# Square and column scaling of the gated SSD rows moved from GpSimd to ScalarE in a hybrid decoder step

## The chip, the cores and the metric

One Trainium2 chip, one core of it. The metric is the device time of one execution in microseconds (us), lower is better. The engines are TensorE (PE in the rows), VectorE (DVE), ScalarE (ACT), GpSimd (POOL) and SyncE (SP), each with its own instruction queue; they meet at semaphores.

## What is computed

One inference step of a one-layer decoder, for a prompt of 256 tokens and 8 samples of 8 new tokens each, so 320 columns in all: a Mamba-2 branch beside a chunked MLP branch, a gated merge, and a mixture of 32 experts (top 4). The change touches the gated norm between the Mamba-2 branch and its output weights:

```python
def rmsnorm(x, w):
    xf = x.astype(jnp.float32)
    y = xf * lax.rsqrt(jnp.mean(xf * xf, axis=-1, keepdims=True) + EPS)
    return (y * w.astype(jnp.float32)).astype(x.dtype)

y_ssd, new_ssm = ssd_chunked(xs, dt, a_log, b_ssm, c_ssm, ssm_init)   # 32 heads of 64 channels
y_ssd = y_ssd + d_skip[:, None] * xs
y_ssd = rmsnorm(y_ssd.reshape(bsz, l, D_INNER) * jax.nn.silu(z), gnorm_w)
merged = g_ssd * (y_ssd @ w_branch_ssd) + g_mlp * (y_mlp @ w_branch_mlp)
h = x + merged @ w_out
```

Everything is float32. Weights and activations of the mixer are split into a rounded high part (fp32r) and the rest, and multiplied as three products.

## The kernel before

**Stages.** The kernel runs on one core in one program. From 0 to about 118 us it norms and turns the input and projects the first column tiles. The pair stage (about 118 to 369 us) handles the 32 heads as 16 pairs of 128 channels, j = 0 to 15, in four groups g of four; jj = j % 4. The branch stage follows (L1189 on), in which the MLP and SSD branches meet their weights, then the output projection, the router, and from about 600 us the experts, whose weights stream in on SyncE's queue. SyncE issues the first expert loads when all eight merged tiles are there (L597).

**Layout.** Channels lie on the 128 partitions and the 320 tokens along the row. yT holds 16 tiles of 128x320: first silu(z), then, multiplied in place, the gated y of pair j. The norm over channels needs the sum of the squares of all 16 tiles, kept in sqacc (128x320), which one matmul with ones adds up over the partitions after the last pair (L1211). The norm's weight is a column per tile, gn_col[:, j].

**One pair.** The order of every engine's queue is written out by hand. TensorE (L1159 to L1187) makes the heads' cumulated decays (heads, L1083), turns the input states (turn_state, in two halves), multiplies the diagonal block of the pair before, makes chunk states, new states (L1136) and the off-diagonal part (offT), and between these the halves of two or three projection tiles that the table beside(j) names (half_tile: L900 to L909): convolution tiles, z tiles, in the last group u tiles and a gate. The heads of pair j wait for the head decays of pair j-1 (e_ready) and its sample states (sn_ready). ScalarE (L1839 to L1870) reads the last tile of the pair before (late), then copies states (L1769), takes the exponentials (read_heads, exponent), copies chunk states (L1778, L1781), makes the high part of the late tile's weights (L1628), issues the stores of the states and the load of the input states for pair j+1 (store_states, on ScalarE's own DMA queue), copies offT (L1861) and reads the next tiles: for a convolution tile raw (L1688, L1689) and a scaled copy (L1691). VectorE (L2364 to L2385) makes the segments of pair j (L2307), the gated y of pair j-1 (gated, L2338 to L2342), the convolution of the late tile (three taps, a 128x256 and a 128x64 step each, L2222 and L2224), the weighted x (L2276), the low part of the late weights (L2086), the sample states (L2319), and further convolutions. The low part of a weight tile is made four tiles ahead of its use by TensorE (split_lo).

**GpSimd** (L785 to L800) masks the decays of pair j (decay, L756, 128x640), then handles pair j-1's y in squares (L759): square (L763 or L765), sum into sqacc (L766), and y times the norm's column in place (L767), chained by semaphores. Then it packs the convolution rows (L734, L735), copies prefixes (L723) and in each group stores rows by its own DMA queue. After the last pair it waits for the partition sum and issues the router's and biases' loads.

**After the pairs** ScalarE makes the high parts of the operands in the order of BRANCH (L522): the MLP rows, weight 2, four quarters of y, the other weights (split_high, L1818, copies at L1836). Quarter i of y waits for sq_ready at 4i+4, since its rows must be scaled before they are split. VectorE makes the low parts in the same order (split_low, L2362).

Of the kernel before, what the change touches and what calls it, by code (L numbers as in the profile page):

```python
# [12 lines left out]
ALU = mybir.AluOpType  # L13
# [16 lines left out]
PAIRS = DI // P  # L30
# [90 lines left out]
def build(nc, x_prompt, x_sample, state_conv, state_ssm, norm_mix, w_in, conv_w, conv_b, dt_bias, a_log,  # L121
# [4 lines left out]
    with ctx:  # L126
# [160 lines left out]
        def part(*shape):  # L287

            n = 1
            for d in shape:  # L290
# [76 lines left out]
                 "sT_psum", "sT_ready", "s0_ready", "sf_psum", "sf_ready", "sn_psum", "sn_ready",  # L367
                 "off_psum", "off_read", "yd_psum", "y_ready", "sq_ready", "sq_psum", "rs_var", "rs_std",
                 "rs_ready", "gates_ready", "merged", "out_psum", "h_ready", 
# [285 lines left out]
        def _(pool):  # L655
# [102 lines left out]

            def squares(j):  # L759

                pool.wait_ge(S["y_ready"], j + 1)
                if j == 0:
                    link(pool.tensor_tensor(sqacc, yT[:, j, :], yT[:, j, :], ALU.mult))  # L763
                else:
                    link(pool.tensor_tensor(sq, yT[:, j, :], yT[:, j, :], ALU.mult))  # L765
                    link(pool.tensor_tensor(sqacc, sqacc, sq, ALU.add))  # L766
                pool.tensor_scalar(yT[:, j, :], yT[:, j, :], gn_col[:, j:j + 1], None, ALU.mult  # L767
                                   ).then_inc(S["sq_ready"], 1)

# [15 lines left out]
            for j in range(PAIRS):  # L785
                convs = [n for kind, n in beside(j) if kind == "conv"]
                if convs:
                    prefix_of(convs[0])
                if j % 4 == 0:
                    mask_b(j // 4)  # L790
                decay(j)
                if j:
                    squares(j - 1)
                for i, n in enumerate(convs):
                    if i:
                        prefix_of(n)
                    pack_of(n)
                if j % 4 == 0:
                    store_rows(j // 4)
            squares(PAIRS - 1)  # L800
            pool.wait_ge(s_new_out[0], 16 * PAIRS // 2)
# [802 lines left out]
        def _(act):  # L1604
# [178 lines left out]
            def exponent(j):  # L1783
# [4 lines left out]
                fn(dec, seg, ACT.Exp).then_inc(S["exp_ready"], 1)  # L1788

            def store_states(j):  # L1790

# [26 lines left out]
            def split_high(item):  # L1818
# [8 lines left out]
                if kind == "y":  # L1827
                    act.wait_ge(s_new_out[0], 16 * PAIRS // 2)
                    act.wait_ge(s_new_out[1], 16 * PAIRS // 2)
                    act.wait_ge(s_fin_out[0], 16 * PAIRS // 2)  # L1830
                    act.wait_ge(s_fin_out[1], 16 * PAIRS // 2)
                    act.wait_ge(S["yd_psum"], PAIRS)
                    act.wait_ge(S["sq_ready"], 4 * i + 4)
                if kind == "mlp":
# [4 lines left out]
            for j in range(PAIRS):  # L1839
# [10 lines left out]
                read_state(j, 1)  # L1850
                read_chunk_states(j)
                if jj >= 2 and after_g < G:
                    read_rows(after_g, jj - 2)
# [33 lines left out]
            for item in BRANCH:  # L1887
                kind, i = item
                split_high(item)
                if item == ("w", 4):  # L1890
                    act.wait_ge(S["rs_var"], 1)
                    act.sqrt(rstd_row, rstd_row).then_inc(S["rs_std"], 1)
                if kind == "w" and i % 5 == 2:
# [170 lines left out]
        def _(dve):  # L2064
# [336 lines left out]
            for item in BRANCH:  # L2401
# [4 lines left out]
                if item == ("w", 4):  # L2406
                    dve.wait_ge(S["sq_psum"], 1)
                    dve.tensor_scalar(rstd_row, bank[0][:, 0:T], 1.0 / DI, EPS, ALU.mult, ALU.add
                                      ).then_inc(S["rs_var"], 1)
                    dve.wait_ge(S["rs_std"], 1)  # L2410
                    dve.reciprocal(rstd_row, rstd_row).then_inc(S["rs_ready"], 1)
                    dve.wait_ge(S["rs_ready"], 1)
# [345 lines left out]
```

## Time and profile before

| | |
|---|---|
| median of 3 runs | 1535.34 us (1534.7 to 1537.41) |
| the profiled execution | 1537.08 us |
| its span in the trace | 1535.2 us |
| TensorE busy | 1424.8 us (93%) |
| VectorE busy | 602.3 us (39%) |
| ScalarE busy | 381.1 us (25%) |
| GpSimd busy | 202.4 us (13%), 303 instructions |
| mean granted TensorE clock | 0.981 of full speed |
| chain that ended last | PE 60%, DMA 25%, DVE 8%, ACT 1%, POOL 1% |

The span runs from the first to the last instruction; 1.9 us lie around it. The profiled execution is 1.7 us above the median of the runs. In the rows, idle time before an instruction is that of its own engine, and the releaser is the instruction whose semaphore came last. Start times are us from the span's start. In merged rows (xN) the length is that of the N instructions together.

### The profile page before, as it was taken

What the parts mean: (1) busy time and instruction counts of PE and PEld (TensorE: products, weight loads), DVE (VectorE), ACT (ScalarE), POOL (GpSimd) and SP (SyncE); (2) the same over time, 40 slices, a digit from 0 to 9 for tenths busy, and PEclk for the clock granted to TensorE, in tenths of its full rate; (3) what the DMA queues carried; (4) which work ended last, traced back from release to release, by engine and by line L of the source; (5) the groups of instructions that cost most, each with busy time, mean ns of one, the idle gap of its engine ahead of it and who ended that gap; (6) DMA issues with size and microseconds to landing.
All of it is one profiled execution on the core that took longest, in us unless ns stands there. A gap on an engine that the chain in (4) does not pass through costs nothing.

```text
span 1535.2 us, 22060 instructions
## 1 busy us (share of the span) xinstructions
PE 1424.8 (93%) x8519; PEld 830.7 (54%) x8520; DVE 602.3 (39%) x1348; ACT 381.1 (25%) x642; POOL 202.4 (13%) x303
## 2 busy tenths in 40 slices
PE   5999999999999999989999899987999989999996
PEld 4988788788999544434434434432434434434432
DVE  4796888967544152312212212202212113112213
ACT  4556676756332141001001001000000001001002
POOL 4023444335930000000000000000000000000000
PEclk9999999999999999999999999998999999999999
DMA  7443554555444879999999999997999999999996
GB/s 225 147 136 112 145 166 124 170 154 158 148 155 151 328 290 387 427 428 429 427 429 428 429 428 429 428 427 290 406 429 428 429 428 429 428 429 429 429 422 238
DMA packets 127406, 495.85 MB, mean 323 GB/s; under 512 B 7300, under 2 KB 95420, under 8 KB 102200
## 3 DMA queue, kind: packets, MB, share of 16 engines
q1 hardware_dynamic: 89152, 471.75, 76.0%
q10 hardware_dynamic: 35888, 18.88, 4.2%
q0 software_dynamic: 2304, 4.40, 1.0%
q8 instruction: 40, 0.66, 0.2%
q14 instruction: 22, 0.18, 0.0%
HBM read 483.65 MB, written 11.34 MB: 322 GB/s over the span
## 4 chain that ended last, share of the span: by engine, by line
PE 60%; DMA 25%; DVE 8%; issue 3%; SPq 2%; ACT 1%; POOL 1%; DVEq 0%; ACTq 0%; POOLq 0%
DMA ring_b<-in_w_gu 23%; PE bank L1405 18%; PE bank L1488 9%; PE bank L1227 7%; PE bank L1342 3%; PE bank L900 3%; PE bank L909 3%; PE bank L881 3%; PE bank L1243 2%; PE bank L905 2%; PE bank L902 1%; DVE ring_r L2086 1%; SPq L583 1%; DVE arena L2222 1%; DVE arena L2224 1%
## 5 line engine op out<-in xcount | busy, mean ns | idle before, releaser
L1405 PE MATMUL bank<-ring_b,xe 128*64 128x512 f32 x1248 | 346.2, 618 | 36.6 <-DMA ring_b<-in_w_gu 36.5
L1405 PEld LDWEIGHTS bank<-ring_b,xe 128*64 128x64 f32 x1248 | 113.9, 142 | 253.3 <-issue 252.6
L1405 PE MATMUL bank<-ring,xe 128*64 128x512 f32 x768 | 226.0, 594 | 5.0 <-DMA ring<-in_w_gu 4.7
L1488 PE MATMUL bank<-ring,actT 128*64 128x512 f32 x720 | 213.0, 596 | 0.0
L1608 ACT ACTIVATE swi<-swi 128x256 f32<-128x256 f32 x66 | 27.3, 416 | 560.5 <-DVE swi L2535 528.1
L2535 DVE TENSOR_SCALAR swi<-bank 128x256 f32<-128x256 f32 x60 | 25.5, 425 | 314.5 <-PE bank L1405 309.7
L1227 PE MATMUL bank<-rounded,ring_r 128*128 128x320 f32 x912 | 133.7, 308 | 1.7 <-DVE ring_r L2362 1.7
L1227 PEld LDWEIGHTS bank<-rounded,ring_r 128*128 128x128 f32 x912 | 132.8, 188 | 2.6 <-DVE ring_r L2362 2.4
L853 POOL TENSOR_TENSOR kept<-take 128x256 bf16<-128x256 bf16 x15 | 9.2, 612 | 855.2 <-PE bank L1470 855.2
L1405 PEld LDWEIGHTS bank<-ring,xe 128*64 128x64 f32 x768 | 74.6, 137 | 76.4 <-issue 76.4
L1488 PE MATMUL bank<-ring_b,actT 128*64 128x512 f32 x240 | 105.8, 593 | 4.3 <-ACT actT L1970 4.3
L2576 DVE TENSOR_TENSOR hid<-hid,bank 128x512 f32<-128x512 f32 (+1 forms) x90 | 57.8, 682 | 115.0 <-PE bank L1366 115.0
L1488 PEld LDWEIGHTS bank<-ring,actT 128*64 128x64 f32 x720 | 64.6, 137 | 59.1 <-issue 58.8
L900 PE MATMUL bank<-rounded,ring_r 128*128 128x320 f32 x456 | 84.1, 328 | 0.6 <-ACT rounded L1634 0.6
L909 PE MATMUL bank<-rounded,ring_r 128*128 128x320 f32 x456 | 76.6, 310 | 0.0
L2086 DVE TENSOR_TENSOR ring_r<-ring,ring_r 128x1024 fp32r<-128x1024 f32 (+1 forms) x61 | 73.7, 1222 | 3.5 <-ACT ring_r L1628 3.3
L881 PE MATMUL bank<-ident,arena 128*128 128x128 f32 (+5 forms) x337 | 55.8, 285 | 19.0 <-DVE arena L2079 17.8
L900 PEld LDWEIGHTS bank<-rounded,ring_r 128*128 128x128 f32 x456 | 70.5, 196 | 3.6 <-issue 2.3
L909 PEld LDWEIGHTS bank<-rounded,ring_r 128*128 128x128 f32 x456 | 69.8, 189 | 0.0
L2669 DVE SCALAR_TENSOR_TENSOR ye_lo<-bank,routing,ye_hi 128x512 fp32r<-128x512 f32 x32 | 22.6, 747 | 115.4 <-ACT ye_hi L1981 105.7
L1488 PEld LDWEIGHTS bank<-ring_b,actT 128*64 128x64 f32 x240 | 31.6, 137 | 60.6 <-issue 60.6
L1628 ACT CAST ring_r<-ring 128x1024 fp32r<-128x1024 f32 (+1 forms) x61 | 63.4, 1041 | 1.6 <-ACT arena L1608 1.0
(371 smaller groups left out, 2016.4 us busy)
## 6 DMA issues: line engine op xcount, KB each, us to landing
ring_b<-in_w_gu SPq DMA_DIRECT2D x79, 2048.0 KB, 16.5
ring<-in_w_gu SPq DMA_DIRECT2D x49, 2048.0 KB, 16.7
ring<-in_w_down SPq DMA_DIRECT2D x47, 2048.0 KB, 18.7
ring<-in_w_in SPq DMA_DIRECT2D x32, 1024.0 KB, 5.4
ring_b<-in_w_down SPq DMA_DIRECT2D x15, 2048.0 KB, 14.4
arena<-in_state_ssm ACTq DMA_DIRECT2D x16, 512.0 KB, 4.7
out<-arena ACTq DMA_DIRECT2D x16, 512.0 KB, 3.6
ring<-in_w_branch_ssd SPq DMA_DIRECT2D x8, 1024.0 KB, 5.2
```

Of the source, the lines that this page charges most:

```text
L881: return pe.transpose(out, in_, ident[0:in_.shape[0], 0:in_.shape[0]])
L900: pe.matmul(o, w_h[k], hn_hi[:, k, :], start=(k == 0), stop=False)
L905: pe.matmul(o, w_l[k], hn_hi[:, k, :], start=False, stop=False)
L909: mm = pe.matmul(o, w_h[k], hn_lo[:, k, :], start=False, stop=(k == KD - 1))
L1227: mm = pe.matmul(bank[4 * m + b][:, 0:T], w[:, k, m * P:m * P + P], v[:, k0 + k, :], start=(k == 0 and which != 4 and v is x_h and w is w_ ...
L1243: mm = pe.matmul(bank[2 * half + c][:, :], mergedT[:, 2 * m + k, tok(c)], w[:, k, hb(c, half)], start=(m == 0 and k == 0), stop=(m == 3 an ...
L1342: mm = pe.matmul(bank[6 + k // 4][:, (k % 4) * P:(k % 4) * P + P], part[0:rows(c), c, k * P:k * P + P], chosen_rows[0:rows(c), c, :], star ...
L1405: mm = pe.matmul(bank[q][side(h), :], xe[:, j, side(h)], moe_slot(2 * i + h, first)[:, 2 * FF * k + 512 * q:2 * FF * k + 512 * q + 512], s ...
L1488: mm = pe.matmul(bank[4 + half][side(h), :], actT[:, f, side(h)], w[:, D * k + 512 * half:D * k + 512 * half + 512], start=False, stop=(f ...
L1628: act.copy(hi, w).then_inc(S["split_hi"], 1)
L2086: dve.tensor_tensor(lo, w, hi.bitcast(F32), ALU.subtract).then_inc(S["split_lo"], 1)
L2576: dve.tensor_tensor(hid[0:rows(c), c, hb(c, half)], hid[0:rows(c), c, hb(c, half)], bank[6 + i % 2][0:rows(c), :], ALU.add).then_inc(S["cm ...
```

## The change

ScalarE makes the square of pair j's gated y and its scaling by the norm's column (square_y). GpSimd keeps the decay mask and the sum (add_squares). The square of pair 0 is written straight to sqacc. ScalarE's instruction for pair j-1 stands in pair j behind its chunk states; that of pair 15 stands ahead of the high part of the last quarter of y. ScalarE waits for GpSimd's sum of the pair before, since sq has one buffer, and for its own square before it scales in place. GpSimd waits for both. The square root of the norm uses the count of another semaphore pair (ln_var, ln_std) in place of its own.

```diff
--- before.py
+++ after.py
@@ -365,7 +365,7 @@
                  "cb_psum", "cb_ready", "bt_psum", "bt_ready", "bm_ready", "xt_psum", "xw_ready",
                  "head_psum", "seg_ready", "exp_ready", "decay_ready", "e_ready", "ident_ready", "mlp_ready",
                  "sT_psum", "sT_ready", "s0_ready", "sf_psum", "sf_ready", "sn_psum", "sn_ready",
-                 "off_psum", "off_read", "yd_psum", "y_ready", "sq_ready", "sq_psum", "rs_var", "rs_std",
+                 "off_psum", "off_read", "yd_psum", "y_ready", "sq_ready", "sq_psum", "y_squared",
                  "rs_ready", "gates_ready", "merged", "out_psum", "h_ready", 
                  "lg_psum", "lg_ready", "ge_ready", 
                  "split_hi", "split_lo", "cnt_psum", "rank_psum", "work_ready", 
@@ -756,16 +756,14 @@
                 pool.tensor_tensor(dec, dec, cbm.unsqueeze(1).to_broadcast([P, 2, T]), ALU.mult
                                    ).then_inc(S["decay_ready"], 1)
 
-            def squares(j):
-
-                pool.wait_ge(S["y_ready"], j + 1)
-                if j == 0:
-                    link(pool.tensor_tensor(sqacc, yT[:, j, :], yT[:, j, :], ALU.mult))
+            def add_squares(j):
+
+                pool.wait_ge(S["y_squared"], 2 * j + 2)
+                if j:
+                    pool.wait_ge(S["sq_ready"], j)
+                    pool.tensor_tensor(sqacc, sqacc, sq, ALU.add).then_inc(S["sq_ready"], 1)
                 else:
-                    link(pool.tensor_tensor(sq, yT[:, j, :], yT[:, j, :], ALU.mult))
-                    link(pool.tensor_tensor(sqacc, sqacc, sq, ALU.add))
-                pool.tensor_scalar(yT[:, j, :], yT[:, j, :], gn_col[:, j:j + 1], None, ALU.mult
-                                   ).then_inc(S["sq_ready"], 1)
+                    pool.sem_inc(S["sq_ready"], 1)
 
             def store_rows(g):
 
@@ -790,14 +788,14 @@
                     mask_b(j // 4)
                 decay(j)
                 if j:
-                    squares(j - 1)
+                    add_squares(j - 1)
                 for i, n in enumerate(convs):
                     if i:
                         prefix_of(n)
                     pack_of(n)
                 if j % 4 == 0:
                     store_rows(j // 4)
-            squares(PAIRS - 1)
+            add_squares(PAIRS - 1)
             pool.wait_ge(s_new_out[0], 16 * PAIRS // 2)
             pool.wait_ge(s_new_out[1], 16 * PAIRS // 2)
             pool.wait_ge(s_fin_out[0], 16 * PAIRS // 2)
@@ -1787,6 +1785,15 @@
                     act.wait_ge(S["yd_psum"], j)
                 fn(dec, seg, ACT.Exp).then_inc(S["exp_ready"], 1)
 
+            def square_y(j):
+
+                act.wait_ge(S["y_ready"], j + 1)
+                if j:
+                    act.wait_ge(S["sq_ready"], j)
+                fn(sq if j else sqacc, yT[:, j, :], ACT.Square).then_inc(S["y_squared"], 1)
+                act.wait_ge(S["y_squared"], 2 * j + 1)
+                act.mul(yT[:, j, :], yT[:, j, :], gn_col[:, j:j + 1]).then_inc(S["y_squared"], 1)
+
             def store_states(j):
 
                 p = j % 2
@@ -1830,6 +1837,8 @@
                     act.wait_ge(s_fin_out[0], 16 * PAIRS // 2)
                     act.wait_ge(s_fin_out[1], 16 * PAIRS // 2)
                     act.wait_ge(S["yd_psum"], PAIRS)
+                    if i == 3:
+                        square_y(PAIRS - 1)
                     act.wait_ge(S["sq_ready"], 4 * i + 4)
                 if kind == "mlp":
                     act.wait_ge(S["mlp_ready"], KD)
@@ -1849,6 +1858,8 @@
                     read_b(j // 4)
                 read_state(j, 1)
                 read_chunk_states(j)
+                if j:
+                    square_y(j - 1)
                 if jj >= 2 and after_g < G:
                     read_rows(after_g, jj - 2)
                 if j:
@@ -1888,8 +1899,8 @@
                 kind, i = item
                 split_high(item)
                 if item == ("w", 4):
-                    act.wait_ge(S["rs_var"], 1)
-                    act.sqrt(rstd_row, rstd_row).then_inc(S["rs_std"], 1)
+                    act.wait_ge(S["ln_var"], 4)
+                    act.sqrt(rstd_row, rstd_row).then_inc(S["ln_std"], 1)
                 if kind == "w" and i % 5 == 2:
                     gates_of("gs", i // 5)
                 if kind == "w" and i % 5 == 3:
@@ -2406,8 +2417,8 @@
                 if item == ("w", 4):
                     dve.wait_ge(S["sq_psum"], 1)
                     dve.tensor_scalar(rstd_row, bank[0][:, 0:T], 1.0 / DI, EPS, ALU.mult, ALU.add
-                                      ).then_inc(S["rs_var"], 1)
-                    dve.wait_ge(S["rs_std"], 1)
+                                      ).then_inc(S["ln_var"], 1)
+                    dve.wait_ge(S["ln_std"], 4)
                     dve.reciprocal(rstd_row, rstd_row).then_inc(S["rs_ready"], 1)
                     dve.wait_ge(S["rs_ready"], 1)
             merge(3)
```

## Rows read from the trace of the kernel before

**Rows 1.** Busy us by stage (PE, PEld, DVE, ACT, POOL); clock, DMA share, GB/s.

```profile
300.00:350.00 50.00, 48.38 (x366) 42.00 (x366) 36.55 (x98) 30.17 (x51) 17.48 (x19) 0.97 0.52 154
...
600.00:1535.00 935.00, 855.45 (x4602) 353.88 (x4598) 215.69 (x489) 76.26 (x159) 14.43 (x30) 0.98 0.98 414
```

**Rows 2.** Timeline, TensorE: start, us, engine, line, operation [idle before, releaser].

```profile
178.39 0.52 PE L1083 MATMUL bank<-rounded,rounded 64*128 64x320 f32 x2 [1.64 <-issue]
...
291.40 0.53 PE L1083 MATMUL bank<-rounded,rounded 64*128 64x320 f32 x2 [0.27 <-issue]
...
296.96 0.40 PE L881 MATMUL bank<-ident,arena 128*27 128x128 f32 x2 [0.20 <-ACT arena L1608]
...
306.73 0.53 PE L1083 MATMUL bank<-rounded,rounded 64*128 64x320 f32 x2 [1.62 <-issue]
```

**Rows 3.** Timeline, VectorE, pairs 8 (alone) and 10.

```profile
257.25 0.48 DVE L2222 SCALAR_TENSOR_TENSOR arena<-arena 128x256 f32<-128x256 f32 x1
257.65 0.28 DVE L2224 SCALAR_TENSOR_TENSOR arena<-arena 128x64 f32<-128x64 f32 x1
...
282.58 1.58 DVE L2224 SCALAR_TENSOR_TENSOR arena<-arena 128x64 f32<-128x64 f32 x1
284.19 0.84 DVE L2222 SCALAR_TENSOR_TENSOR arena<-arena 128x256 f32<-128x256 f32 x1
...
285.88 0.78 DVE L2222 SCALAR_TENSOR_TENSOR arena<-arena 128x256 f32<-128x256 f32 x1
...
291.23 0.47 DVE L2222 SCALAR_TENSOR_TENSOR arena<-arena 128x256 f32<-128x256 f32 x1
```

**Rows 4.** Timeline, all engines, end of the pairs.

```profile
373.36 2.81 DVE L2362 TENSOR_TENSOR ring_r<-ring,ring_r 128x2048 fp32r<-128x2048 f32 x1
...
377.00 3.53 POOL L767 TENSOR_SCALAR arena<-arena 128x320 f32<-128x320 f32 x1
380.64 1.26 ACT L1836 CAST rounded<-arena 128x1280 fp32r<-128x1280 f32 x1 [3.35 <-POOL arena L767]
...
381.93 1.49 DVE L2362 TENSOR_TENSOR rounded<-arena,rounded 128x1280 fp32r<-128x1280 f32 x1 [0.62 <-ACT rounded L1836]
...
383.74 2.29 DVE L2362 TENSOR_TENSOR ring_r<-ring,ring_r 128x2048 fp32r<-128x2048 f32 x1 [0.32 <-ACT ring_r L1836]
...
386.09 21.25 PE L1227 MATMUL bank<-rounded,ring_r 128*128 128x320 f32 x144 [0.80 <-DVE ring_r L2362]
```

**Rows 5.** GpSimd by line, 118 to 382 us: busy, mean ns, idle.

```profile
L767 POOL TENSOR_SCALAR arena<-arena 128x320 f32<-128x320 f32 x16 | 24.4, 1523 | 1.6
...
L765 POOL TENSOR_TENSOR arena<-arena 128x320 f32<-128x320 f32 x15 | 13.3, 887 | 5.4 <-DVE arena L2342 5.4
```

**Rows 6.** Timeline, ScalarE, pairs 9 and 10.

```profile
272.02 0.37 ACT L1861 COPY arena<-bank 128x256 f32<-128x256 f32 x1 [1.02 <-PE bank L1148]
...
273.95 0.37 ACT L1688 COPY arena<-bank 128x256 f32<-128x256 f32 x1 [0.24 <-PE bank L909]
...
290.03 0.63 ACT L1608 ACTIVATE arena<-bank,arena 128x320 f32<-128x320 f32 x1
```

**Rows 7.** Busy time behind the gaps, pairs 4 and 12, as rows 1.

```profile
178.39:183.48 5.09, 5.09 (x41) 4.31 (x42) 4.53 (x14) 3.26 (x5) 0.00 (x0) 1.00 0.72 194
...
306.73:313.32 6.59, 6.59 (x41) 5.42 (x42) 4.62 (x14) 3.26 (x5) 0.00 (x0) 0.74 0.46 156
```

**Rows 8.** ScalarE by line, 118 to 370 us; line 1981: minimum, median, maximum.

```profile
L1608 ACT ACT_TABLE_LOAD x30 | 38.5, 1283 | 0.5
L1769 ACT COPY arena<-bank 128x512 f32<-128x512 f32 x31 | 18.2, 586 | 23.3 <-PE bank L881 22.8
...
L1608 ACT ACTIVATE arena<-arena 128x320 f32<-128x320 f32 x18 | 7.8, 467 | 0.1
...
L1981 ACT ACTIVATE ye_hi<-bank,routing x30: 680/684/687, 605.5 to 1466.5; 128x512 fp32r<-128x512 f32 x30
```

**Rows 9.** DMA issues of the page: KB each, us from issue to landing.

```profile
arena<-in_state_ssm ACTq DMA_DIRECT2D x16, 512.0 KB, 4.7
```

## The prediction, made before the changed kernel ran

> **What bounds the kernel now.** I read the busy times by stage first. From 600 us on the DMA engines are busy 0.98 of the time at 414 GB/s, so that stage is as long as its bytes and only its start can move. In the pair stage (about 118 to 369 us) no DMA bound is near: TensorE is busy 48.4 of 50 us, VectorE 36.6, ScalarE 30.2, GpSimd 17.5 [rows 1]. So the whole question is whether TensorE's way from 118 us to the start of the MoE loads gets shorter; what it gains there should reach the end one for one, since the loads wait for the merged rows.
>
> The chain of waits leaves TensorE in two places there, and the timelines say why. One is each group of four pairs: TensorE stands still for 1.6 us before the heads of pairs 4, 8 and 12, and 0.27 and 0.20 us before that in pair 11 (pairs 3 and 7 look the same) [rows 2]. The heads wait for VectorE's sample states, and VectorE is late because its convolution collides with GpSimd: the 128x256 step takes 0.48 us alone and 0.84 or 0.78 next to GpSimd, the 128x64 step 0.28 alone and 1.58 [rows 3]. The other place is the end of the pairs: the last square, sum and scaling on GpSimd are all that ScalarE's fourth high copy of y waits for [rows 4].
>
> **What is removed.** GpSimd loses per pair the square (0.887 us mean) and the scaling (1.523 us mean) and keeps the sum [rows 5]. Over 15 and 16 of them that is 38 us of GpSimd time, nearly all beside other work. Only its effect on VectorE and the last pair count.
>
> Take pair 10. Between 282.58 and 286.66 VectorE's convolution ran in turn against the decay mask, the square, the sum and the scaling. The first 128x64 step lost 1.58-0.28 = 1.30 us to the decay, which stays. The second 128x256 step lost 0.84-0.48 = 0.36 to the square and the third lost 0.78-0.48 = 0.30 to the scaling [rows 3]; those 0.66 us go. The 0.6 us that the 128x64 step between them lost to the sum stays, because ScalarE delivers the square at about 284.3, still inside this convolution; had the sum come later, 1.26 us would go. So 0.66 per contended convolution, ends 0 and 1.26.
>
> In pair 10 the gain is cut: the next convolution started at 291.23 [rows 3], and its input is finished by ScalarE at 290.03+0.63 = 290.66 [rows 6], a time that hangs on TensorE. So 0.57 of it arrives. It takes out TensorE's 0.27 and 0.20 us of pair 11 [rows 2]. Pair 11 has the same collision, another 0.66. Together VectorE reaches the heads of pair 12 1.2 us earlier (0.57+0.66), and TensorE's gaps of 0.27+0.20+1.62 = 2.09 us can take all of it. Three groups do this (pairs 2-3, 6-7, 10-11): **3 x 1.2 = 3.6 us** (ends 0 and 3 x 1.8 = 5.4).
>
> **TensorE's clock.** Behind the gap before pair 12 the granted clock averages 0.74 over the first 41 matmuls (it is at 1.2 GHz for half of the time and then back at 2.4), and they take 6.59 us; pair 8 is the same. Behind the equally long gap before pair 4 it stays at 1.00, and the same 41 take 5.09 [rows 7]. A fall costs 1.5 us. With the gaps cut from 1.6 to about 0.9 us a fall is less likely. Ends 0 and 3.0; one gap of three kept its clock even at 1.6 us, so I take one of the two falls: **1.5 us**.
>
> **What is added.** ScalarE gets a Square and a multiplication by a column, both SBUF to SBUF over 128x320. A ScalarE function of that form takes 0.467 us. The factor from a column costs 0.10 more, as a 128x512 from PSUM shows with it (0.684) and without (0.586), so 0.56 for the second [rows 8]. Between them ScalarE waits for its own semaphore, some 0.05 us. Sum 1.08 us in pairs 1 to 15, about 1.0 with the overlap of neighbours. No DMA issue is added; the state stores and the reload of the input states behind it in ScalarE's queue go out 1 us later. The reload issued at 284.31 in pair 10 is used first at 291.86 and lands in 4.7 us [rows 9], so 2.8 us are spare there, the least of a group, and 1.8 stay.
>
> What hides it: ScalarE idles 1.02 us before its offT copy in pair 9 [rows 6]; in the other pairs it idles there as long or longer (up to 2.8). In pair 9 the 1.0 just fits. Behind it stands 0.24 us more, the idle time before the convolution's input is read at 273.95 [rows 6], and that read starts the very VectorE chain that is late in pairs 10 and 11. If the two instructions cost over 1.26 us, each 0.1 us more is lost in each group. VectorE's split of the late tile waits for ScalarE's cast, now 1 us later, so the split and the sample states slip some 0.5 us in pairs of the first and second kind; VectorE idles 1 us behind them before it needs TensorE again, which covers it. In pair 15 alone the cover is short: the split for the last gate tile ends at about 364.4, TensorE wanted it at 364.3: **0.1 us lost**.
>
> The wait for y itself hides: in pair 10 y is written at 282.3, ScalarE comes to it at 283.2. The wait of ScalarE for GpSimd's previous sum lies a pair back. GpSimd's sum now waits for ScalarE, with the packing of the next tile behind it; it ends by about 270.3 in pair 9 and the packing starts at 274.6.
>
> **The end of the pairs.** Before, GpSimd had the last y at 370.80 and ended at 380.53, since its three instructions waited for VectorE's low parts (the scaling took 3.53 us where its mean is 1.523); the fourth copy of y followed at 380.64 after 3.35 us of idle time [rows 4]. Now ScalarE squares and scales behind its third copy, from 377.2 to 378.3, and only the sum is left. VectorE began the low part of the first branch weight at 373.36, in 2.81 us; without GpSimd such a part takes 2.29, and a quarter of y 1.49 (1.4 from start to start) [rows 4]. So its second quarter ends at 373.36+2.29+2.8 = 378.4. If the sum gets in there it is done at 379.1; if VectorE's third quarter goes first, at 380.5. The copy starts at 379.2 or 380.6: 1.4 us earlier, or nothing. Of GpSimd's last three instructions before, two got in at the first end of a VectorE instruction and the third, called at 377.00, at the second. TensorE was free at 383.49 and started the next block at 386.09 [rows 4], 0.8 of it spent on the sum over partitions, so up to 1.8 us can be used. I take **1.0 us** (ends -0.2 and 1.8).
>
> The square root of the norm only changes its semaphores: 0.
>
> **Sum:** 3.6+1.5+1.0-0.1 = 6.0 us off the profiled execution's 1537.08, so 1531.1. The median of the runs shown is 1.7 us lower, and the forecast is of a median: 1535.3-6.0 = 1529.3 us. A measurement of this kernel can tell about 0.2% (3.1 us) from no change.
>
> **Rivals.** *The relief is eaten up* (no change). Sum and decay go on holding VectorE, ScalarE's two instructions cost more than 1.26 us and the convolution's input comes late. For: the cover is met within 0.02 us in pair 9. Against: every ScalarE time there is known. The groups then give 0 to 1 us and the end as much: 1534 us. Chance 0.25.
>
> *The clock stays up everywhere* and the sum falls outside the convolutions: 5.4+3.0+1.4 = 9.8 us, 1525.5. For: one of three equal gaps already kept the clock. Against: ScalarE's timing in pair 10 puts the sum inside. Chance 0.18.
>
> *ScalarE becomes the bound* (slower). No row shows a Square right behind an Exp. If it needs its own table, each pair gets one more load of 1.283 us [rows 8], ScalarE's addition is 2.3 us against little more than 1.02 of idle time, and some 1.2 us run over in eight pairs (1, 3, 5, 7, 9, 11, 12, 13). From a cost of about 1.26 us a pair it bites. Carried to TensorE: 8 x 1.2 - 4.5 = +5, 1540.3 us. For: between Exp and Silu the kernel loads one each time (30 in the stage). Against: Squares elsewhere in the kernel run without a load of their own, behind a Sigmoid and before and after a square root.
>
> The Trainium skill, ScalarE: Activation LUTs, What ACT_TABLE_LOAD costs, puts a switch of tables at about 2.66 us, a drain included. The rows show 1.283 with hardly any idle time at the load; by the page's figure this rival would cost another 1.4 us in each pair, and be at about 1551. The same page (Table sets) says that cheap functions are in every set, without naming Square; by that the rival falls away.
>
> **Chances.** Forecast 0.50, eaten up 0.25, clock and relief in full 0.18, ScalarE bound 0.07. Of the forecast's own case about nine tenths lie beyond 3.1 us. Faster 0.63, same 0.29, slower 0.08. The range takes in the full relief below and no change above: 1525.5 to 1535.5.
>
> **What would show it.** GpSimd's 128x320 work down to 15 sums; the gaps before the heads of pairs 4, 8 and 12 about 0.9 us instead of 1.6, or gone, and the granted clock behind them; the third 128x256 step of pairs 10 and 11 back at 0.48; ScalarE's idle time before offT near 0 in pair 9; the fourth copy of y at 1.4 us less or unchanged behind the last y. Wrong would be: table loads above 30 in the pair stage, new idle time of TensorE behind ScalarE, or gaps of 1.6 us that stay.

## The result, and the profile after

The changed kernel took 1526.09 us (median of 7 runs, 1524.35 to 1530.53) against 1535.47 us (7 runs, 1534.7 to 1537.41) for the kernel before, measured beside it: 9.4 us less by the medians, 8.8 by the ratio of 0.9943 [0.9927, 0.9959]. The changed kernel's runs fall into two clusters, four of 1524.35 to 1526.09 and three of 1530.01 to 1530.53 us, so its median hangs on a single run. The forecast was 1529.3 us, range 1525.5 to 1535.5. A second measurement (below) gave 1528.93 against 1535.89, ratio 0.9952 [0.9936, 0.9967]. The profiled execution took 1524.53 us, 12.55 less than the one of before.

The page of the changed kernel, its head and the engines' busy time:

```profile
span 1522.8 us, 22090 instructions
...
PE   1417.0 (93%) x8519; PEld 825.2 (54%) x8520; DVE 596.6 (39%) x1348; ACT 395.4 (26%) x674; POOL 160.3 (11%) x271
```

GpSimd lost 42.1 us of busy time and ScalarE gained 14.3, yet the span fell by 12.4. Neither engine is a bound, so their totals say nothing; the stages do. Busy time by stage, changed kernel (columns as in [rows 1]):

```profile
118.00:370.00 252.00, 248.72 (x1926) 214.03 (x1925) 207.13 (x538) 188.91 (x337) 66.50 (x103) 1.00 0.53 156
600.00:1522.00 922.00, 842.94 (x4548) 350.39 (x4544) 213.29 (x480) 74.93 (x157) 14.43 (x30) 0.98 0.98 414
```

The expert stage is what it was (0.98 of the DMA engines' time, 414 GB/s). All but at most 0.6 us (below) of what the kernel won, it won before that stage. The granted clock of the pair stage is now 1.00.

**TensorE's gaps.** Timeline of TensorE, changed kernel, the heads of pairs 4, 8 and 12, against [rows 2]:

```profile
173.10 0.52 PE L1081 MATMUL bank<-rounded,rounded 64*128 64x320 f32 x2 [0.99 <-issue]
...
235.46 0.53 PE L1081 MATMUL bank<-rounded,rounded 64*128 64x320 f32 x2 [0.98 <-issue]
...
297.84 0.53 PE L1081 MATMUL bank<-rounded,rounded 64*128 64x320 f32 x2 [0.99 <-issue]
```

The gaps shrank from 1.63 to 0.99 us, and those of 0.27 and 0.20 us in pairs 3, 7 and 11 are gone. Behind the heads the same 41 matmuls as in [rows 7] (windows of the changed kernel; all three alike):

```profile
235.46:240.55 5.09, 5.09 (x41) 4.30 (x42) 4.51 (x14) 3.26 (x5) 0.00 (x0) 1.00 0.81 209
297.84:302.93 5.09, 5.09 (x40) 4.30 (x41) 4.51 (x14) 3.26 (x5) 0.00 (x0) 1.00 0.70 211
```

They take 5.09 us at a clock of 1.00 (the 2.4 GHz level), where they took 6.59 at 0.74 behind two of the three gaps before.

**VectorE and GpSimd in pair 10.** GpSimd beside the steps of [rows 3], kernel before, the square, the sum and the scaling:

```profile
284.04 0.72 POOL L765 TENSOR_TENSOR arena<-arena 128x320 f32<-128x320 f32 x1
284.83 0.92 POOL L766 TENSOR_TENSOR arena<-arena 128x320 f32<-128x320 f32 x1
285.85 1.08 POOL L767 TENSOR_SCALAR arena<-arena 128x320 f32<-128x320 f32 x1
```

Timeline of VectorE and then of GpSimd, changed kernel:

```profile
274.74 1.58 DVE L2235 SCALAR_TENSOR_TENSOR arena<-arena 128x64 f32<-128x64 f32 x1
276.36 0.49 DVE L2233 SCALAR_TENSOR_TENSOR arena<-arena 128x256 f32<-128x256 f32 x1
276.76 0.90 DVE L2235 SCALAR_TENSOR_TENSOR arena<-arena 128x64 f32<-128x64 f32 x1
277.69 0.48 DVE L2233 SCALAR_TENSOR_TENSOR arena<-arena 128x256 f32<-128x256 f32 x1
...
282.95 0.48 DVE L2233 SCALAR_TENSOR_TENSOR arena<-arena 128x256 f32<-128x256 f32 x1
```

```profile
274.59 1.65 POOL L756 TENSOR_TENSOR arena<-arena 128x640 f32<-128x640 f32 x1 [2.62 <-ACT arena L1606]
276.50 1.07 POOL L764 TENSOR_TENSOR arena<-arena 128x320 f32<-128x320 f32 x1 [0.27 <-ACT arena L1795]
```

Two instructions are left to collide. The decay mask still stretches the first 128x64 step to 1.58 us; the sum stretches the second to 0.90, 0.62 above the 0.28 that it takes alone. The second and third 128x256 steps, 0.84 and 0.78 before, are back at 0.49 and 0.48.

**ScalarE.** Its groups by line, 118 to 368 us, changed kernel (busy us, mean ns | idle before):

```profile
L1606 ACT ACT_TABLE_LOAD x31 | 39.8, 1283 | 0.5
...
L1795 ACT ACTIVATE arena<-arena 128x320 f32<-128x320 f32 x16 | 9.0, 564 | 0.5
...
L1872 ACT COPY arena<-bank 128x256 f32<-128x256 f32 x16 | 6.0, 372 | 12.7 <-PE bank L1146 12.4
```

Its timeline in pairs 9 and 10:

```profile
264.18 0.37 ACT L1872 COPY arena<-bank 128x256 f32<-128x256 f32 x1
...
266.11 0.37 ACT L1686 COPY arena<-bank 128x256 f32<-128x256 f32 x1 [0.25 <-PE bank L907]
...
275.33 0.49 ACT L1606 ACTIVATE arena<-arena 128x320 f32<-128x320 f32 x1
275.86 0.56 ACT L1795 ACTIVATE arena<-arena 128x320 f32<-128x320 f32 x1
...
282.19 0.63 ACT L1606 ACTIVATE arena<-bank,arena 128x320 f32<-128x320 f32 x1
```

Square (0.49) and scaling (0.56, as estimated) stand behind the exponentials without a table load. The 31st load in this window is the one ahead of the sigmoid behind pair 15, which lay outside the window of [rows 8]. The offT copy of pair 9 has lost all of its 1.02 us of idle time [rows 6]; the 0.24 us behind it are intact (0.25).

**The end of the pairs.** Timeline of all engines, changed kernel, against [rows 4]; the instruction that makes the last y starts at 359.85 (before: 370.22):

```profile
365.19 6.46 DVE L2373 TENSOR_TENSOR rounded<-arena,rounded 128x1280 fp32r<-128x1280 f32 x4
...
366.79 0.48 ACT L1606 ACTIVATE arena<-arena 128x320 f32<-128x320 f32 x1
367.31 0.56 ACT L1795 ACTIVATE arena<-arena 128x320 f32<-128x320 f32 x1
367.95 0.88 POOL L764 TENSOR_TENSOR arena<-arena 128x320 f32<-128x320 f32 x1 [15.34 <-ACT arena L1795]
368.87 1.26 ACT L1845 CAST rounded<-arena 128x1280 fp32r<-128x1280 f32 x1 [0.99 <-POOL arena L764]
...
374.32 3.90 PE L1225 MATMUL bank<-rounded,ring_r 128*128 128x320 f32 x25 [0.77 <-DVE ring_r L2373]
```

The last sum took 0.88 us; it got in between two of VectorE's four quarters, which together took 6.46. The high copy of the fourth quarter starts 9.02 us behind the last y, where it was 10.42 (380.64 - 370.22), and the block that started 15.87 behind it (386.09 - 370.22) starts at 14.47 (374.32 - 359.85).

**Where the 12.4 us of span came from**, by these landmarks: 1.3 us ahead of the heads of pair 0 (113.03 to 111.76), 3.0 in pair 0, where the clock fell behind a gap of 1.2 us in the trace of before and not in this one, 1.1, 2.5 and 2.5 in the three groups from the heads of pair 1 to those of pair 13 (63.43, 64.92, 64.92 to 62.36, 62.38, 62.38), nothing up to the last y, 1.4 at the end of the pairs, 0.6 in all that follows. The first two, 4.2 us (1.27 and 2.96), lie in code that the change leaves as it was. They are the luck of two single executions: in all kernels run here the way from the heads of pair 0 to those of pair 1 is 16.7, 18.2 or 19.6 us, in no order with what was changed. So the experiments are compared by the length of the three groups and by the start of that block behind the last y ("the end", below), and by their runs.

### The profile page after: what moved, and what is told of

Its sections match the earlier page's. It is cut to its first block, busy times and chain, and to the rows that moved or that the text cites. A ratio compares the mean times of both kernels' runs of the same rounds, so it can differ in the third digit from the quotient of the medians.

```text
span 1522.8 us, 22090 instructions
## 1 busy us (share of the span) xinstructions
PE 1417.0 (93%) x8519; PEld 825.2 (54%) x8520; DVE 596.6 (39%) x1348; ACT 395.4 (26%) x674; POOL 160.3 (11%) x271
## 4 chain that ended last, share of the span: by engine, by line
PE 61%; DMA 26%; DVE 5%; issue 3%; ACT 2%; SPq 2%; POOL 0%; DVEq 0%; ACTq 0%; POOLq 0%
DMA ring_b<-in_w_gu 25%; PE bank L1403 18%; PE bank L1486 8%; PE bank L1225 7%; PE bank L898 3%; PE bank L907 3%; PE bank L1340 3%; PE bank L879 3%; PE bank L1241 2%; PE bank L903 2%; PE bank L900 2%; SPq L583 1%; PE bank L1134 1%; DMA ring<-in_w_down 1%; PE bank L1541 1%
## 5 line engine op out<-in xcount | busy, mean ns | idle before, releaser
L879 PE MATMUL bank<-ident,arena 128*128 128x128 f32 (+5 forms) x337 | 54.6, 280 | 18.2 <-DVE arena L2090 17.3
## 6 DMA issues: line engine op xcount, KB each, us to landing
ring_b<-in_w_down SPq DMA_DIRECT2D x15, 2048.0 KB, 14.5
```

The lines of the kernel that those rows point to most:

```text
L879: return pe.transpose(out, in_, ident[0:in_.shape[0], 0:in_.shape[0]])
```

## The experiments

The theory was that the gain comes from VectorE: without GpSimd's square and scaling its convolution is shorter, TensorE's gaps shrink, and the clock comes back with them; ScalarE's share is hidden. Rivals were that it lies at the end of the pairs, or in chance.

**The end alone.** Pair 15 as in the change, pairs 0 to 14 on GpSimd.

```diff
-            squares(PAIRS - 1)
+            pool.wait_ge(S["y_squared"], 2)
+            pool.tensor_tensor(sqacc, sqacc, sq, ALU.add).then_inc(S["sq_ready"], 1)
...
+                    if i == 3:
+                        j = PAIRS - 1
+                        act.wait_ge(S["y_ready"], PAIRS)
+                        act.wait_ge(S["sq_ready"], j)
+                        fn(sq, yT[:, j, :], ACT.Square).then_inc(S["y_squared"], 1)
+                        act.wait_ge(S["y_squared"], 1)
+                        act.mul(yT[:, j, :], yT[:, j, :], gn_col[:, j:j + 1]).then_inc(S["y_squared"], 1)
...
```

> Only pair 15's square and scaling go to ScalarE; pairs 0 to 14 stay on GpSimd. Theory (three separate gains: 1.05 us a group, the clock, 1.4 us at the end): the gaps before the heads of pairs 4, 8 and 12 stay at 1.6 us, the start of the block of weight 3 comes 1.4 us earlier behind the last y, and the total is 1.0 to 1.6 us below the kernel before. Rival (the end gives nothing by itself, all comes from the groups): no change behind the last y, total within 0.5 us of before.

Measured: 1535.53 us, ratio 1.0 [0.999, 1.0009]; groups 64.95, 64.91, 64.89; the end at 15.85 (386.47 - 370.62). Timelines of VectorE, GpSimd and ScalarE, a stretch of each:

```profile
375.97 4.29 DVE L2370 TENSOR_TENSOR rounded<-arena,rounded 128x1280 fp32r<-128x1280 f32 x3
```

```profile
378.74 2.25 POOL L801 TENSOR_TENSOR arena<-arena 128x320 f32<-128x320 f32 x1 [12.96 <-ACT arena L1840]
```

```profile
381.02 1.26 ACT L1844 CAST rounded<-arena 128x1280 fp32r<-128x1280 f32 x1 [2.36 <-POOL arena L801]
```

The prediction had left this open: whether the sum gets in ahead of VectorE's third quarter of y. In the changed kernel's trace it did (0.88 us); here it did not. VectorE went through three quarters without a break, and the sum, started at 378.74, took 2.25 us. The third quarter began at about 378.77 (two steps of 1.4 us behind 375.97), within 0.04 us of the sum's start. The gain of 1.4 us did not come.

**The pairs alone.** Pairs 0 to 14 as in the change, pair 15 on GpSimd.

```diff
-            add_squares(PAIRS - 1)
+            pool.wait_ge(S["y_ready"], PAIRS)
+            pool.wait_ge(S["sq_ready"], PAIRS - 1)
+            link(pool.tensor_tensor(sq, yT[:, PAIRS - 1, :], yT[:, PAIRS - 1, :], ALU.mult))
+            link(pool.tensor_tensor(sqacc, sqacc, sq, ALU.add))
+            pool.tensor_scalar(yT[:, PAIRS - 1, :], yT[:, PAIRS - 1, :], gn_col[:, PAIRS - 1:PAIRS], None, ALU.mult
+                               ).then_inc(S["sq_ready"], 1)
...
-                    if i == 3:
-                        square_y(PAIRS - 1)
```

> Pairs 0 to 14 on ScalarE, pair 15 as before on GpSimd. Theory: gaps before the heads of pairs 4, 8 and 12 near 1.0 us, the groups of four pairs 62.4 us long (before: 63.4, 64.9, 64.9), the end of the pairs as before; total 1.4 us above the changed kernel where both have the same granted clock. Rival (the last pair carries it): total as before.

Measured: 1528.17 us, ratio 0.9948 [0.993, 0.9966]; groups 62.42, 62.38, 62.38; gaps 0.99, 0.98, 1.00; clock 1.00 behind all; the end at 15.9. The groups are those of the change. Whether the total lies 1.4 us above the changed kernel, as expected, can't be read: the changed kernel was not measured beside this one.

**The relief without ScalarE's share.** Squares and scalings of pairs 1 to 14 are left out on every engine; the sums stay, over zeros.

```diff
+            link(pool.memset(sq, 0.0))
...
+                if 0 < j < PAIRS - 1:
+                    pool.wait_ge(S["sq_ready"], j)
+                    pool.tensor_tensor(sqacc, sqacc, sq, ALU.add).then_inc(S["sq_ready"], 1)
+                    return
+                if j == PAIRS - 1:
+                    pool.wait_ge(S["sq_ready"], j)
```

> Squares and scalings of pairs 1 to 14 are left out altogether (the norm then lacks them, and those rows their column factor); GpSimd keeps the sums, ScalarE gets nothing. Theory (GpSimd's hold on VectorE is what was relieved, ScalarE's share is free): the groups are 62.4 us long, as in the changed kernel, and the gaps 1.0 us; the end as before. Rival (ScalarE's 1 us a pair costs something that the changed kernel pays): groups shorter than 62.2 us.

Measured: 1527.59 us, ratio 0.9952 [0.9933, 0.9971]; groups 62.29, 62.26, 62.25; gaps 0.86, 0.87, 0.86. With ScalarE's share a group is 0.11 us longer (62.37, means of three). Most of that is the place of GpSimd's sum: it no longer waits for ScalarE, so it meets VectorE's second 128x256 step and stretches it by 0.52 us (from 0.48), where in the change it costs the 128x64 step behind it 0.62. Timeline of VectorE, pair 10:

```profile
276.15 1.00 DVE L2229 SCALAR_TENSOR_TENSOR arena<-arena 128x256 f32<-128x256 f32 x1
```

So ScalarE's two instructions are hidden, but for the moment at which they let the sum go.

**GpSimd's load given back.** The changed kernel, with a product and a one-tensor multiplication on GpSimd again in pairs 1 to 14. They work on sq, so the sum adds fourth powers.

```diff
-                if j:
+                if 0 < j < PAIRS - 1:
+                    pool.wait_ge(S["sq_ready"], j)
+                    link(pool.tensor_tensor(sq, sq, sq, ALU.mult))
+                    link(pool.tensor_tensor(sqacc, sqacc, sq, ALU.add))
+                    pool.tensor_scalar(sq, sq, 1.0, None, ALU.mult).then_inc(S["sq_ready"], 1)
+                elif j:
```

> The changed kernel, and GpSimd again does a product of two tensors and a one-tensor multiplication of 128x320 per pair beside the sum in pairs 1 to 14 (the norm then sums fourth powers). Theory (the two GpSimd instructions cost VectorE 0.66 us in each contended convolution): gaps back at about 1.6 us, groups at 63.4 us where the clock stays and 64.9 where it falls; 3 to 6 us slower than the changed kernel. Rival (the gain came from ScalarE's new order or from chance): groups stay at 62.4 us.

Measured: 1535.47 us, ratio 0.9996 [0.9987, 1.0006]; groups 65.00, 64.94, 64.96. Timelines of GpSimd and VectorE in pair 10, and the busy time behind the heads of pairs 4 and 8:

```profile
282.60 0.92 POOL L764 TENSOR_TENSOR arena<-arena 128x320 f32<-128x320 f32 x1 [0.27 <-ACT arena L1800]
283.59 0.86 POOL L765 TENSOR_TENSOR arena<-arena 128x320 f32<-128x320 f32 x1
284.54 1.06 POOL L766 TENSOR_SCALAR arena<-arena 128x320 f32<-128x320 f32 x1
```

```profile
282.85 0.74 DVE L2240 SCALAR_TENSOR_TENSOR arena<-arena 128x64 f32<-128x64 f32 x1
283.63 1.10 DVE L2238 SCALAR_TENSOR_TENSOR arena<-arena 128x256 f32<-128x256 f32 x1
284.66 0.46 DVE L2240 SCALAR_TENSOR_TENSOR arena<-arena 128x64 f32<-128x64 f32 x1
```

```profile
175.11:181.70 6.59, 6.59 (x40) 5.75 (x41) 4.51 (x14) 3.26 (x5) 0.00 (x0) 0.74 0.56 152
240.08:246.67 6.59, 6.59 (x41) 5.75 (x42) 4.55 (x14) 3.26 (x5) 0.00 (x0) 0.74 0.57 153
```

With ScalarE's share in place as in the change, GpSimd's two instructions alone take the whole gain of the groups back. The three VectorE steps shown lose 0.46, 0.62 and 0.18 us, 1.26 in sum; in the change the convolution loses 0.62 behind the mask, and in the kernel before 0.36, 0.60 and 0.30, again 1.26. The gaps are 1.67, 1.66 and 1.67 us again, and the clock fell behind all three. This and the two runs before it settle where the groups' time comes from.

**The changed kernel again**, measured on the same chip as the next two experiments and as ScalarE's share raised, below.

> The changed kernel unaltered, for a second trace. Theory (the last sum's place behind the last y is a toss between GpSimd and VectorE, 0.04 us apart): groups again at 62.4 us; the block of weight 3 starts either 14.5 or 15.9 us behind the last y. Rival (the change gains 1.4 us there every time): 14.5.

Measured: 1528.93 us (1527.38 to 1530.78), ratio 0.9952 [0.9936, 0.9967]; groups 62.38, 62.41, 62.37; gaps 0.98 three times; way from pair 0 to pair 1 18.24; the end at 15.9. Timelines of VectorE and GpSimd:

```profile
367.80 4.29 DVE L2373 TENSOR_TENSOR rounded<-arena,rounded 128x1280 fp32r<-128x1280 f32 x3
```

```profile
370.56 2.26 POOL L764 TENSOR_TENSOR arena<-arena 128x320 f32<-128x320 f32 x1 [15.35 <-ACT arena L1795]
```

The same program as in the first trace, and the last sum took 2.26 us where it took 0.88. The groups come back to 0.03 us; the end does not.

**The sum made to wait for the late convolution.**

```diff
                 pool.wait_ge(S["y_squared"], 2 * j + 2)
+                late = beside(j)[-1] if j + 1 < PAIRS else None
+                if late and late[0] == "conv":
+                    pool.wait_ge(S["conv_done"], late[1] + 1)
```

> The changed kernel, but in the pairs with a late convolution tile GpSimd's sum waits until that convolution is done. Theory (the sum still costs VectorE 0.6 us inside the convolution): the 128x64 step beside it falls from 0.90 to 0.28 us, gaps before the heads of pairs 4, 8 and 12 from 0.99 to about 0.4 us, groups 61.8 us, 1.8 us less in total. Rival (the gap has another cause by now): groups stay at 62.4.

Measured: 1525.26 us, ratio 0.993 [0.9914, 0.9945]; groups 61.75, 61.76, 61.76; gaps 0.35 to 0.37; the end at 15.9. 0.62 us a group, which is what the 128x64 step loses to the sum (0.90 - 0.28). That is 1.9 us in the three groups. The medians lie 3.7 us apart, so the groups explain half of it. In the two traces the way from pair 0 to pair 1, which is unchanged code, differs by another 1.6 us (16.68 and 18.24).

**The decay mask made to wait too, and VectorE's third quarter of y for the last sum.**

```diff
                 pool.wait_ge(S["cb_ready"], j // 4 + 1)
+                late = beside(j - 1)[-1] if j else None
+                if late and late[0] == "conv":
+                    pool.wait_ge(S["conv_done"], late[1] + 1)
...
                 v, hi, lo = branch_item(item)
+                if item == ("y", 2):
+                    dve.wait_ge(S["sq_ready"], PAIRS)
```

> As the late sum, the decay mask waits for the late convolution too, and at the end VectorE's third quarter of y waits for the last sum. Theory (all of the remaining gap is GpSimd's hold; TensorE's own work in a group is 61.4 us; the end always gains 1.4 us): gaps gone, groups 61.4 us, the block of weight 3 14.5 us behind the last y, in total 3 us below the changed kernel in its best runs. Rival (GpSimd's work only moves to the low part of the late weights and holds VectorE there): groups 61.8 us or more.

Measured: 1522.74 us (1521.29 to 1527.42), ratio 0.9917 [0.9903, 0.9931]; groups 61.34, 61.34, 61.36; no gap before the heads of pairs 4, 8 and 12; the end at 14.5. Timelines of VectorE and GpSimd, pair 10 and the end:

```profile
275.79 0.28 DVE L2241 SCALAR_TENSOR_TENSOR arena<-arena 128x64 f32<-128x64 f32 x1
...
276.51 0.28 DVE L2241 SCALAR_TENSOR_TENSOR arena<-arena 128x64 f32<-128x64 f32 x1
...
368.89 2.89 DVE L2381 TENSOR_TENSOR rounded<-arena,rounded 128x1280 fp32r<-128x1280 f32 x2 [0.79 <-POOL arena L770]
```

```profile
277.68 1.56 POOL L759 TENSOR_TENSOR arena<-arena 128x640 f32<-128x640 f32 x1 [4.65 <-DVE arena L2241]
...
367.98 0.88 POOL L770 TENSOR_TENSOR arena<-arena 128x320 f32<-128x320 f32 x1 [15.35 <-ACT arena L1801]
```

No step of the convolution is stretched. Of the mask's 1.30 us only the 0.36 that was left of the gap could be had, since TensorE then runs through; and the last sum goes first by order and not by luck. This version beats both kernels on the same chip: 13.2 us below the one before in the medians, and below the changed one by 6.2 in the medians, 4.9 in the means (its five runs lie at 1521.29 to 1522.74 and at 1526.56 and 1527.42) and 4.5 by the landmarks of the two traces (3.1 in the groups, 1.4 at the end).

**ScalarE's share raised.** The Square made three times in pairs 0 to 14, so 2.1 us a pair and not 1.08.

```diff
-                pool.wait_ge(S["y_squared"], 2 * j + 2)
+                pool.wait_ge(S["y_squared"], 4 * j + (4 if j + 1 < PAIRS else 2))
...
-                fn(sq if j else sqacc, yT[:, j, :], ACT.Square).then_inc(S["y_squared"], 1)
-                act.wait_ge(S["y_squared"], 2 * j + 1)
+                for i in range(3 if j + 1 < PAIRS else 1):
+                    fn(sq if j else sqacc, yT[:, j, :], ACT.Square).then_inc(S["y_squared"], 1)
+                    act.wait_ge(S["y_squared"], 4 * j + i + 1)
```

> The changed kernel with every Square of pairs 0 to 14 done three times, 1.0 us more for ScalarE in each pair (about 2.1 us instead of 1.08). Theory (beyond 1.26 us a pair ScalarE delays the convolution's input, 0.8 us in each group): groups 63.2 us, gaps before the heads near 1.0 to 1.8 us, and 64.7 where the clock falls behind them. Rival (ScalarE has more room than 1.26 us): groups stay at 62.4 us.

Measured: 1531.16 us, ratio 0.9968 [0.9957, 0.9978]; groups 62.83, 62.92, 62.93; gaps 1.05 to 1.06 and new ones of 0.19 to 0.33 before the heads of pairs 3, 7 and 11. Half a microsecond a group, between the two expectations (63.2 and 62.4): beyond the slack ScalarE costs, but less than the excess of some 0.8 us, and the clock stayed up. In pair 9 the read of the convolution's input starts 0.61 us later behind the heads than in the change (13.53 and 12.92 us), and 0.54 of it reach the group. In pair 10 the sum, 1 us later too, meets the last 128x64 step (0.96 us) and costs it 0.68 in place of 0.62, so this run raises GpSimd's hold a little as well.

**A long gap with a light GpSimd.** The changed kernel, two weighings of VectorE made twice in pairs 4, 8 and 12, to tell what the clock falls behind: the gap, or GpSimd's load.

```diff
+                if j % 4 == 0 and j:
+                    link(by_head(xw[:, p, :], 2, 0, 2, P))
+                    link(by_head(xf[:, p, :], 3, 0, 1, P))
```

> The changed kernel with two of VectorE's weighings (128x256 and 128x128 from PSUM, 0.7 us together) done twice for pairs 4, 8 and 12; GpSimd and ScalarE do what they do in the changed kernel. Theory (the length of the gap before the heads alone decides on the clock): gaps of 1.6 to 1.7 us, the granted clock falls behind most of them, and those groups are 64.5 to 64.7 us long, the others 63.0 to 63.2. Rival (the clock stayed in the changed kernel for another reason, such as GpSimd's lighter load): no fall, all three groups 63.0 to 63.2 us.

Measured: 1535.57 us, ratio 0.9993 [0.9983, 1.0003]; gaps 1.76, 1.75, 1.75; groups 64.71, 63.14, 64.63. Busy time behind the three heads:

```profile
174.73:181.32 6.59, 6.59 (x40) 5.81 (x41) 4.46 (x14) 3.26 (x5) 0.00 (x0) 0.74 0.57 153
239.43:244.52 5.09, 5.09 (x41) 4.30 (x41) 4.51 (x14) 3.26 (x5) 0.00 (x0) 1.00 0.72 195
302.58:309.17 6.59, 6.59 (x41) 5.42 (x42) 4.62 (x14) 3.26 (x5) 0.00 (x0) 0.74 0.45 154
```

A long gap is enough, without GpSimd's load: with GpSimd as light as in the change the clock fell behind two of three, at 1.5 us each. 0.76 us more of standing still cost 2.3 us in the groups where it fell and 0.76 in the one where it did not. The groups are 2.3 us shorter in sum than in the second trace of before (192.5 to 194.7), and the runs 1.3 (up to 2.6).

**The end alone, with the order fixed.** The first experiment plus the wait of VectorE's third quarter.

```diff
...
+                if item == ("y", 2):
+                    dve.wait_ge(S["sq_ready"], PAIRS)
...
```

> Only pair 15 on ScalarE as in tail_only, and VectorE's third quarter of y waits for the last sum, which decides the toss for GpSimd. Theory: block of weight 3 at 14.5 us behind the last y instead of 15.9, groups 63.4 or 64.9 as before, 1.4 us below the kernel before. Rival (a later wait takes the place, as TensorE's next weight): 14.5 us there, but nothing in the total.

Measured: 1535.09 us, ratio 0.9994 [0.9984, 1.0003] (the kernel before beside it: 1536.89); groups 64.95, 64.91, 64.94; the end at 14.5 (382.0 - 367.5). The trace has its 1.4 us; the runs show 1.8 less in the medians, which is inside what they can tell from nothing.

**The kernel before, traced a second time.**

> The kernel before, for a second trace. Theory: gaps of 1.6 us before the heads of pairs 4, 8 and 12, the clock falls behind two or three of them (groups of 64.9 us), block of weight 3 at 15.9 us behind the last y. Rival (the falls in the first trace were chance): groups of 63.4 us in the main.

Measured: 1535.72 us, span 1533.9; groups 64.91, 64.89, 64.94; gaps 1.62, 1.62, 1.65, the clock down behind all three; way from pair 0 to pair 1 16.67; the end at 15.9. The one gap of three that kept its clock in the first trace was the exception.

## Why the prediction was right, point by point

**Relief of VectorE (3.6 us, 1.2 a group): right.** Pair 10 came out as written down: the mask's 1.30 us stayed, 0.36 and 0.30 went, and the 0.6 us of the sum stayed (0.62). A group without a fall of the clock went from 63.43 to 62.37 us, 1.06. The whole is 3 x 1.06 = 3.2 us. Most of what is missing to 1.2 lies in pair 10. The prediction let the next convolution start when ScalarE had finished its input (290.66), 0.57 us before it did. But GpSimd's copy of the prefix stands between (timelines of GpSimd, kernel before and changed kernel):

```profile
290.55 0.21 POOL L723 COPY arena<-arena 128x24 f32<-128x24 f32 x1
```

```profile
282.70 0.21 POOL L723 COPY arena<-arena 128x24 f32<-128x24 f32 x1
```

It ended at 290.76 before, under VectorE's other work, and ends at 282.91 in the change, 0.04 us ahead of the convolution. Counted from the heads of pair 10 (277.59 and 269.75) the convolution starts at 13.64 us before (291.23) and at 13.20 in the change (282.95): 0.44 arrived and not 0.57. That this relief is GpSimd's square and scaling, and nothing else in the change, is shown by the run that gave two such instructions back. The Trainium skill, SBUF — State Buffer, Who interferes with whom, says that a VectorE instruction with two inputs in SBUF contends with a GpSimd instruction that reads SBUF, at a shared pair of ports that is an exclusive lock. The trace agrees: 1.58 us for a step of 0.28 beside a mask of 1.65, and 0.28 again with the mask behind it.

**The clock (1.5 us): mechanism right, size too small.** This is the term that was mis-sized. It took the one trace for the rule, in which one of three gaps kept the clock, and gave the change one of two falls. Over the kernels here the clock fell behind 16 of 18 gaps of 1.62 to 1.76 us (both traces of before, the two that changed only the end, the given-back load and the VectorE delay, three gaps each), and behind none of 18 gaps of 0.35 to 1.06 us (the change twice, pairs alone, relief alone, the late sum, ScalarE raised). So, by an estimate from these counts, the change removes nearly three falls from the kernel before: 16/18 x 3 x 1.5 = 4.0 us (3.8 by the two traces of before alone, 5 of 6), and 3.0 in the pair of profiles at hand.

**ScalarE's share hidden in the pairs: right.** Measured were 1.05 us (0.49 and 0.56), no new table load, offT's idle time gone in pair 9 and 0.25 us left behind it. The bound of 1.26 us was of the right kind. The price beyond it was put too high: 1.0 us more a pair cost 0.5 a group, where the count gives 0.8.

**The end (1.0 us, either 1.4 or nothing): right as a pair of cases.** It was 1.4 in the first trace of the change and nothing in the second. By the profile's times the sum starts within 0.04 us of a start of VectorE, and which of them goes first changed between executions of one program. Of six traces in which they meet so closely (the change twice, the end alone, the given-back load, the late sum, the VectorE delay) it went first in one; it did in both in which VectorE waits for it. With ScalarE raised it came 0.18 us behind VectorE's third quarter and took 2.04. So the 1.4 us in the first trace of the change are luck.

**Pair 15 (-0.1 us)** did not show: from the heads of pair 13 to the last y it is 44.27 us before and 44.28 after.

**The sum.** 3.2 + 4.0 + (0 or 1.4) is 7.2 to 8.6 us. From 1535.3 that is 1526.7 to 1528.1. The runs say 9.4 by the medians (8.8 by the ratio, with an interval of 6.3 to 11.2) and, in the second measurement, 7.0 (7.4 by the ratio). The first median lies only 0.6 us inside the range; with three of seven runs in the upper cluster, where inside it fell is chance. Of the 12.4 us between the two profiles 4.2 lie in unchanged code and belong to no term; two single profiles tell them from a gain only when they are compared stage by stage.

**The rivals.** *Relief eaten up* is refuted by the groups. *ScalarE the bound* is refuted by the table loads: 31 up to the sigmoid behind pair 15 in both kernels, none of them for a Square. The Trainium skill, ScalarE: Activation LUTs, Table sets, says that cheap functions are in every set, without naming Square; the trace agrees with it for Square. *Clock up everywhere and the sum outside the convolutions* held in its first half and not in its second. Its number, 1525.5, came within 0.6 us of the first measurement, for a sum that stayed inside; the experiment that put the sum outside gained another 0.62 us a group. Both halves together are the late-sum kernel, at 1525.26 where the change took 1528.93, though without the rival's 1.4 us at the end.

**What stays open.** Why the clock falls behind the 1.2 us gap before the heads of pair 0 in five of the thirteen traces was not tried; it is worth 1.5 to 3.0 us. Nor was it tried why those heads start at 111.74 to 113.38 us over all traces, or why what follows the block behind the last y takes 1147.9 to 1151.2, a spread of 3.3 us in no order with what was changed. What spared two of the 18 long gaps is not known, and no gap between 1.06 and 1.62 us was tried before these heads.

## What to carry to other kernels

Before moving work off an idle engine, look at what its instructions hold: here 42 us less on GpSimd mattered, in the groups, only through the 0.66 us by which two of its instructions stretched a late convolution, in two pairs of each group. A wait on the bottleneck's queue that gets shorter can be worth more than its length when the clock falls behind it, so take the clock of several traces, not of one. Where two engines contend and one is late, an explicit wait that puts the helper's instruction behind the late one was worth another 3.1 us in the groups (1.9 for the sum, 1.2 for the mask) on top of moving work away, and it decides a handover at the end that is otherwise left to 0.04 us.

## What was not expected of the hardware

- The length of a gap and the fall of the clock behind it: 16 of 18 at 1.62 to 1.76 us, none of 18 at up to 1.06, five of thirteen at 1.2 (before pair 0, where a fall cost 1.5 or 3.0 us).
- Of two engines that hold each other up the one that starts 0.04 us earlier by the profile's times can still be the one that waits: a GpSimd sum of 0.88 us took 2.26 when a VectorE instruction went in front of it, in one execution and not in another of the same program.
- A Square behind an Exp, and a multiplication by a column (0.56 us for 128x320, against 0.48 for the Square) behind that, ran with no table load and 0.5 us of idle time over all 16.
